# Attention layer of a three-layer fp32 block: softmax rows turned by VectorE in 32x32 blocks and moved by transfers inside SBUF, with the division on ScalarE

## The reference, cut to what matters

```
h  = rmsnorm(x) * (1 + scale) + shift;  proj = h @ w_in      # q, k, v, z
A, heads 0-7 (dense):    s = rope(norm(q)) @ [rope(norm(k)), k_ctx].T * d**-0.5    # 512 x 768
                         o = softmax(s) @ [v, v_ctx]
B, heads 8-15 (window):  each 128-row block of q sees up to 3 neighbouring 128-key blocks, masked,
                         the 256 context keys, and a sink logit that only enters the total
y = concat(oA, oB) * silu(z);  x = x + gate * rmsnorm(y @ w_out)
```

## Time and profile before

| | busy us | share of the span | instructions |
|---|---|---|---|
| span 2534.0 us; median time 2536.99 us | | | 30108 |
| TensorE matmuls (PE) | 2497.7 | 99% | 11975 |
| TensorE weight loads (PEld) | 2020.2 | 80% | 11975 |
| VectorE (DVE) | 1623.8 | 64% | 2444 |
| ScalarE (ACT) | 973.6 | 38% | 1549 |
| GpSimd (POOL) | 110.7 | 4% | 117 |

### The profile page before, as it was taken

How to read it: one execution, slowest core, us unless ns; L and a number is a source line. 1 busy time by engine, 2 the same in 40 slices (tenths; PEclk the granted TensorE clock), 3 DMA queues, 4 the chain that set the end, 5 groups by cost and what they waited for, 6 DMA issues and landing times.

```text
span 2534.0 us, 30108 instructions
## 1 busy us (share of the span) xinstructions
PE 2497.7 (99%) x11975; PEld 2020.2 (80%) x11975; DVE 1623.8 (64%) x2444; ACT 973.6 (38%) x1549; POOL 110.7 (4%) x117
## 2 busy tenths in 40 slices
PE   7999999999999999999999999999999999999999
PEld 4789777777777887888888887888888787887887
DVE  4456776677776768776776768456365577656532
ACT  4232444444444333432434333445455432333421
POOL 0000000000000114000000113000000000000000
PEclk8999999999999999999999999999999999999999
DMA  9955433434433754666645754323222245532342
GB/s 350 336 193 185 127 110 121 125 125 133 132 101 136 258 180 157 208 200 211 200 162 175 249 175 158 111 76 91 80 87 84 75 151 169 175 112 89 123 154 83
DMA packets 293133, 390.58 MB, mean 154 GB/s; under 512 B 11698, under 2 KB 221234, under 8 KB 289154
## 3 DMA queue, kind: packets, MB, share of 16 engines
q1 hardware_dynamic: 287184, 355.84, 43.5%
q0 software_dynamic: 5808, 32.84, 3.5%
q10 hardware_dynamic: 2, 0.00, 0.0%
HBM read 371.85 MB, written 16.78 MB: 153 GB/s over the span
## 4 chain that ended last, share of the span: by engine, by line
PE 89%; DVE 5%; DMA 2%; ACT 2%; issue 1%; SPq 1%; POOL 0%; DVEq 0%; ACTq 0%; POOLq 0%
PE G L2151 74%; PE OB L2151 6%; PE S L2151 6%; PE TB L2154 2%; PE TB L2151 1%; DMA MRAW<-in_ev_mod_w 1%; DMA MORE<-in_ev_mod_w 1%; DVE WLO L1634 1%; DVE MACC L1640 1%; DVE TT L1634 1%; ACT PB L1445 1%; DVE SM L1862 0%; SPq L1129 0%; PE OB L2154 0%; DVE Y L1634 0%
## 5 line engine op out<-in xcount | busy, mean ns | idle before, releaser
L2151 PE MATMUL G<-HHI,WLO 128*128 128x512 f32 x2560 | 1001.0, 391 | 0.0
L2151 PE MATMUL G<-HHI,WHI 128*128 128x512 f32 x1964 | 801.8, 411 | 0.5 <-DVE CLO L1640 0.5
L2151 PE MATMUL G<-HLO,WHI 128*128 128x512 f32 x1928 | 753.2, 391 | 1.6 <-DVE HLO L1640 1.4
L2151 PEld LDWEIGHTS G<-HHI,WLO 128*128 128x128 f32 x2560 | 480.7, 188 | 104.3
L1272 ACT ACTIVATE WHI<-RAW 128x1024 fp32r<-128x1024 f32 x282 | 297.5, 1056 | 560.9 <-PE G L2151 501.6
L1634 DVE TENSOR_TENSOR WLO<-RAW,WHI 128x1024 fp32r<-128x1024 f32 x282 | 344.5, 1222 | 234.9 <-ACT WHI L1272 233.0
L2151 PEld LDWEIGHTS G<-HHI,WHI 128*128 128x128 f32 x1964 | 370.9, 189 | 80.3 <-issue 6.7
L2151 PEld LDWEIGHTS G<-HLO,WHI 128*128 128x128 f32 x1928 | 363.1, 188 | 79.7 <-issue 6.7
L1640 DVE SCALAR_TENSOR_TENSOR MACC<-MWIDE,SC,MACC 128x512 f32<-128x512 f32 x420 | 320.4, 763 | 39.2 <-DMA MWIDE<-in_w_ada 12.8
L2151 PE MATMUL G<-HHI,WHITA 128*128 128x512 f32 x536 | 215.0, 401 | 0.0
L2151 PE MATMUL G<-HLO,WHITA 128*128 128x512 f32 x536 | 209.2, 390 | 0.0
(11 more groups left out here) (347 smaller groups left out, 3060.7 us busy)
## 6 DMA issues: line engine op xcount, KB each, us to landing
RAW<-in_w_in SPq DMA_DIRECT2D x128, 512.0 KB, 3.7
MWIDE<-in_od_mod_w SPq DMA_DIRECT2D x96, 512.0 KB, 4.1
MWIDE<-in_w_ada SPq DMA_DIRECT2D x96, 512.0 KB, 4.6
RAW<-in_ev_w_in SPq DMA_DIRECT2D x80, 512.0 KB, 3.5
RAW<-in_od_w_in SPq DMA_DIRECT2D x64, 512.0 KB, 3.9
MWIDE<-in_ev_mod_w SPq DMA_DIRECT2D x32, 512.0 KB, 3.8
RAW<-in_ev_w_out SPq DMA_DIRECT2D x32, 512.0 KB, 3.3
RAW<-in_od_w_out SPq DMA_DIRECT2D x32, 512.0 KB, 3.3
```

The lines of the kernel that those rows point to most:

```text
L2151: return e.o.matmul(o, l, r, start=start, stop=stop, skip_group_check=True)
```

## The change

The transposes of PB leave TensorE. ScalarE, not VectorE, multiplies a tile by the inverse totals, in place. VectorE then turns each 32x32 block of the tile in place (`transpose` of a 24x32 view). When half a head (two tiles, 256 rows) is turned, SP issues 16 transfers from PB to PT: for each quarter of 32 source partitions `a_` and each residue `r` of the 32-key groups, one of 32 partitions x 6 x 64 elements, that is 192 pieces of 256 B. For 16 heads these are 512 transfers. Columns of PT within a head now lie in another order (quarter, tile, row), which `pv` and `gate` undo with strided views. PB becomes one tensor for a whole head, a half of which may be written again when its transfers have landed. An exponential of a B head with qt < 2 goes out in two instructions, context keys and near keys. Tiles 4 to 7 of a pair come two steps later, and `pv` comes 11 steps after the head's last tile in place of 7. GpSimd's descriptor memory is halved, and WHI gets an ordinary fourth buffer (WHITA and WHIY with their waits go).

```diff
-    WHI3 = [place(f"WHI{i}", [P, 4, 256], F32R)[0] for i in range(3)]
+    WHI = [place(f"WHI{i}", [P, 4, 256], F32R)[0] for i in range(3)]
...
-    PB = [scratch(f"PB{i}", [P, 768], F32, 24 * K1 + i * 3 * K1) for i in range(2)]
+    PB = scratch("PB", [P, 24, P], F32, 24 * K1)
...
+    WHI.append(scratch("WHI3", [P, 4, 256], F32R, 52 * K1))
...
-                later(3 * n, "rows", n)
+                later(3 * n + (2 if n > 3 and p < 7 else 0), "rows", n)
...
-                        later(t + 4 + late, "turn", h, qt, n, 0, not two)
...
-                            later(t + 7, "pv", h)
+                        if qt == 1:
+                            later(t + (6 if i else 4), "turn", h, 0)
+                        elif qt == 3:
+                            later(t + 4, "turn", h, 1)
+                            later(t + 11, "pv", h)
...
+    def p_rows(qt, kt0, kt1):
+        return PB[:, 4 * kt0:4 * kt1, 32 * qt:32 * qt + 32]
...
@@ sp_program @@
+            elif stage == "turn":
+                h, half = a
+                e.wait_ge(v_sm, (h, 2 * half + 1, "turned"))
+                if h:
+                    e.wait_ge(p_pv, h - 1)
+                for a_ in range(4):
+                    src = PB[32 * a_:32 * a_ + 32, :, 64 * half:64 * half + 64].rearrange("p (k r) n -> p k r n", r=4)
+                    for r in range(4):
+                        e.o.dma_start(PT[32 * r:32 * r + 32, :, P * a_ + 64 * half:P * a_ + 64 * half + 64],
+                                      src[:, :, r, :]).then_inc(*ptd[half].up(h, by=16))
...
@@ ScalarE, stage softmax @@
+                if h:
+                    e.wait_ge(ptd[qt // 2], h - 1)
...
+                e.wait_ge(v_sm, (h, qt, "inverse"))
+                cp(p_rows(qt, kt0, 6), p_rows(qt, kt0, 6), SM[:, i + 1:i + 2]).then_inc(*a_exp.up((h, qt, "p")))
@@ VectorE, stage softmax @@
-                e.wait_ge(v_sm, (h, qt, "inverse"))
-                ts(PB[n % 2][:, lo:768], PB[n % 2][:, lo:768], rs, None, MUL).then_inc(*v_sm.up((h, qt, "p")))
+                rows = p_rows(qt, jobs[0][0], 6)
+                e.wait_ge(a_exp, (h, qt, "p"))
+                e.o.transpose(rows, rows).then_inc(*v_sm.up((h, qt, "turned")))
...
@@ TensorE, stages turn and pv @@
-                for x, (j, c0) in enumerate(jobs):
-                    t = tr(bank[:, x * P:(x + 1) * P], PB[n % 2][:, c0:c0 + P])
...
+                e.wait_ge(ptd[0], h)
+                e.wait_ge(ptd[1], h)
...
-    nc = bacc.Bacc("TRN2", target_bir_lowering=False, num_devices=1)
+    nc = bacc.Bacc("TRN2", target_bir_lowering=False, num_devices=1, dynamic_dma_scratch_size=8192)
```

More of the change, by code:

```diff
@@ L185, in build @@
     KHI.append(scratch("KHI3", [P, 768], F32R, 0))
-    QLO = scratch("QLO", [P, 2, SEQ], F32R, 42 * K1)
+    QLO = scratch("QLO", [P, 2, SEQ], F32R, 48 * K1)
     LS2 = [LS, LSB]
@@ L213, in build @@
     xnd = [sig(f"xn{i}") for i in range(6)]
+    ptd = [sig(f"pt{i}") for i in range(2)]
     back = [sig(f"back{i}") for i in range(4)]
@@ L216, in build @@
     last = [sig(f"last{i}") for i in range(4)]
-    sigs = raw + mraw + [par, sel, cst, rope, tri, spill, rcd, dkd] + xnd + back + outd + last
+    sigs = raw + mraw + [par, sel, cst, rope, tri, spill, rcd, dkd] + xnd + ptd + back + outd + last
     def on_chip(*names):
@@ L285, in build @@
     units += out_units(T["od_w_out"][0])
-    third = len(units)
     for p in range(4):
@@ L304, in build @@
         first_chunk.append(first_chunk[-1] + len(u))
[L306 to L317, removed]
     nat = [("c", 0), ("c", 1)] + [("x", i) for i in range(4)]
@@ L731, in pair_task @@
                         put("softmax", h, qt, n)
-                        two = len(score_jobs(h, qt)[1]) > 4
-                        late = 1 if a[0] % 4 == 0 else 0
-                        later(t + 4 + late, "turn", h, qt, n, 0, not two)
-                        if two:
-                            later(t + 5 + late, "turn", h, qt, n, 1, True)
-                        if qt == 3:
-                            later(t + 7, "pv", h)
+                        if qt == 1:
[3 more added lines that the diff above has]
+                            later(t + 11, "pv", h)
                     elif what == "pv":
@@ L745, in pair_task @@
                 yield
+                if p == 7 and t > 28 and last_y < KT - 1:
+                    put("y_split", 1, last_y, h_unit)
+                    last_y += 1
             if p == 7:
-                for k in range(12, KT):
-                    put("y_split", 1, k, h_unit)
-                    yield
+                put("y_split", 1, KT - 1, h_unit)
+                yield
         def first_splits(layer):
@@ L1082, in q_root_of, with by_block @@
         return QROOT[:, h % 2 * 4 + qt:h % 2 * 4 + qt + 1]
-    def runs_of(part):
-        runs = []
-        for x, (j, c0) in enumerate(part):
-            if runs and runs[-1][1] + runs[-1][2] == j:
-                runs[-1][2] += 1
-            else:
-                runs.append([x, j, 1])
-        return runs
+    def p_rows(qt, kt0, kt1):
+        return PB[:, 4 * kt0:4 * kt1, 32 * qt:32 * qt + 32]
+    def by_block(t):
+        return t.rearrange("p (b j) -> p b j", j=32)
     def operand(kind, layer, k):
@@ L1750, in dve_program @@
                 e.wait_ge(a_whi, i)
-                tt(WLO[i % NR][:, :, :], RAW[i % NR][:, :, :], f(whi(i)[:, :, :]), SUB).then_inc(*v_wlo.up(i))
+                tt(WLO[i % NR][:, :, :], RAW[i % NR][:, :, :], f(WHI[i % NS][:, :, :]), SUB).then_inc(*v_wlo.up(i))
             elif stage == "mod_acc":
@@ L2161, in keep_busy @@
             for _ in range(count):
-                mm(G[pair][0][:, :], whi(i)[:, 0, 0:P], HHI[:, KT - 1, :], True, True)
+                mm(G[pair][0][:, :], WHI[i % NS][:, 0, 0:P], HHI[:, KT - 1, :], True, True)
         def token_sums(x, tile, start):
@@ L2304, in pe_program @@
                 layer, u, i, c, t_, pair, last, final = a
-                wh, wl = whi(i), WLO[i % NR]
+                wh, wl = WHI[i % NS], WLO[i % NR]
                 bank = (G[pair] + [OB])[t_ // 2]
```

96 lines of the change are left out of this document (38 added, 58 removed).

## The result

The kernel after takes 2684.67 us (median, 2680.24 to 2687.1), the kernel before beside it 2536.73 us (2535.18 to 2538.44). The ratio is 1.0576, with an interval of 1.0563 to 1.0589: 148 us slower. The forecast was 2565 us, with a range up to 2600. The direction was right and the time was 120 us too short.

What follows compares the result with a forecast made beforehand. TensorE bounds the heads now and loses 37 us; VectorE gets 79 us more against 51.4 us of room and becomes the limit. 2534.0 + 27.6 = 2561.6, with 3 us around it about 2565 us, range 2508 to 2600.

Steps and rivals of the forecast that it cites:

- What bounds the kernel before, and what leaves TensorE: Heads: TensorE busy 277.2 of 280 and 267.2 of 270 us; 336 transposes at 0.11 us leave, 37 us.
- VectorE's new work: Heads' tiles: waiting for ScalarE's multiplication, then turning, adds 41.6 us in A and 37.4 in B, 79 together.
- The sum of 28 us for VectorE: Heads: 79 us more work against 51.4 us of room leaves VectorE needing 27.6 us more than 550.
- SP issues 512 transfers; at 0.37 us each they are 189 us: SP's queue in the heads: a group of 16 takes 5.9 us, SP waits 503 of 550 us; costed at nothing.
- An MWIDE load: Weight loads on SP: issued 11 us ahead, 1.6 us of cover left; if gone, 1 to 2 us in 32 groups.
- So `pv` doesn't wait: Heads: transfers land 13.8 us after a head's last score, and `pv` comes 15.2 us after it.
- ScalarE's wait for the transfers of the head before: ScalarE writing PB: those transfers were issued at least 9.7 us earlier, so costed at nothing.
- The transfers' own cost: DMA engines in the heads: 21 ns per 256 B piece, so a half head takes 4.0 us per engine.
- Rival 3: Transfers land late and `pv` waits, from about 24 ns per piece; 2682 us at 61 ns, 2578 at 40; chance 0.13.
- Rival 1: Heads: VectorE has the room, TensorE keeps the path, all 37 us are won, 2500 to 2503 us; chance 0.20.
- the signs I had named: Heads: TensorE busy about 89%, VectorE's WHI and OB waits nearly vanish, `pv` never waits for transfers' landing.

Runs made afterwards that it cites:

- split: Kernel after with 8 of each 16 transfers issued by SP and 8 by GpSimd: 2572.48 us, 1.0142 of the kernel before.
- few: Kernel after, but from the second head on only 4 of each half head's 16 transfers are issued: 2578.23 us, 1.0166 of the kernel before.
- mwpool: Kernel after with the first layer's MWIDE loads issued by GpSimd, SP keeping all 512 transfers: 2598.09 us, 1.0240 of the kernel before.
- spload: Kernel before plus 512 transfers of the same shape on SP into spare memory nobody reads: 2578.66 us, 1.0164 of the kernel before.
- halfpieces: Kernel after with 96 pieces in place of 192 per transfer from the second head on: 2678.85 us, 1.0558 of the kernel before.

## Why the prediction was wrong, step by step

**What bounds the kernel before, and what leaves TensorE.** Right. All kernels with the transposes gone have 336 matmuls fewer. The 37 us they give back weren't measured by themselves.

**VectorE's new work.** Right in its terms. For 768 columns the wait in front of the turning was put at 1.00 us and is 1.00 (48.2 us in 48 times), and the turning was put at 0.954 us and takes 0.978. ScalarE's multiplication was put at 0.92 us:

```profile
L1865 DVE STREAM_TRANSPOSE PB<-PB 128x768 f32<-128x768 f32 x48 | 47.0, 978 | 48.2 <-ACT PB L1267 48.2
L1865 DVE STREAM_TRANSPOSE PB<-PB 128x640 f32<-128x640 f32 x8 | 6.8, 845 | 7.2 <-ACT PB L1267 7.2
L1865 DVE STREAM_TRANSPOSE PB<-PB 128x512 f32<-128x512 f32 x8 | 5.7, 712 | 6.3 <-ACT PB L1267 6.3
```
```profile
L1267 ACT ACTIVATE PB<-PB,SM x64: 721/936/942, 265.9 to 915.7; 128x768 f32<-128x768 f32 x48, 128x640 f32<-128x640 f32 x8, 128x512 f32<-128x512 f32 x8
```

It is 0.936. One term was sized wrongly: in 16 of the B tiles the turned view spans all six blocks of keys, so 48 tiles and not 32 are turned at full width, which the code states (`p_rows(qt, kt0, 6)`) and I read past. For eight of them that is 0.98 + 1.00 us against 0.71 + 0.79 at 512 columns, for the other eight against 0.85 + 0.90 at 640, together about 6 us.

**The sum of 28 us for VectorE.** Nearly right as a size, and not as a place. Where the transfers are out of the way, 36 us (split) and 42 us (few) are left. TensorE's waits in front of S and for QLO are 48.0 us in split, where the forecast had 65. But from first to last exponential the A heads take 257.5 us before and 258.7 in split, and the B heads 236.2 and 273.2. The forecast had some 12 us of the need in A (41.6 - 29.9) and 16 in B (37.4 - 21.5); the runs show about 1 and 37. Nor did the room go as counted: in split VectorE still waits 24.5 us for WHI. So the size came out near partly by luck, and what makes the B heads dearer is open. The granted clock stood at 0.99 and 0.93 from 250 to 550 and from 550 to 850 us of that kernel; whether the clock took time there, or TensorE had it to spare, no run tells apart.

**"SP issues 512 transfers; at 0.37 us each they are 189 us ... A group of 16 takes 5.9 us and holds up the loads behind it."** This step failed, first in its price. The earlier trace rows show an issue that stands alone. In the trace of before there are also pairs, and the second of a pair takes longer:

```profile
804.44 0.37 SPq L1135 DMA_DIRECT2D RAW<-in_ev_w_out  x1
804.86 0.54 SPq L1143 DMA_DIRECT2D MWIDE<-in_od_mod_w  x1
```

This row of before was to be had. It is still short of the 0.61 us in a streak, but it would have said that 0.37 us is the lower bound and not the price. With 0.65 us the 512 issues are 331 us, and a group is 10.3 to 11.6 us in place of 5.9.

**"An MWIDE load ... 5.9 + 3.5 us to landing leave 1.6 us. If that cover is gone VectorE waits once per group."** This step failed more deeply. The cover was gone, and I priced its loss as a load that comes 1 to 2 us late, and in the sum at nothing. I did not ask what SP's queue itself waits for. An MWIDE load waits for VectorE, and the groups behind it wait too, so a late VectorE makes late transfers, a late `pv`, late transposes of MACC and a later VectorE. The sum "2.5 + 1.9 + 5.9 + 3.5 = 13.8 us after the score, `pv` 15.2 us later" assumed that SP stands ready when a tile is turned. The earlier trace rows said that SP stood waiting for 503 of 550 us. I took them for free time, and they are the time in which a new instruction behind them can't start. Mwpool shows the size of this: 87 us. In place of "So `pv` doesn't wait" the trace has 87.4 us of waits in front of `pv`.

**ScalarE's wait for the transfers of the head before.** Put at nothing, since they were issued at least 9.7 us earlier. They were planned so; in fact they leave late, and ScalarE waits 26.8 us in seven places (rows above).

**The transfers' own cost.** Right, as far as a difference of two pages can tell. A piece was put at 21 ns. In the page after, the queue is busy for 46.0% of 2678.5 us:

```profile
q1 hardware_dynamic: 393680, 381.04, 46.0%
```

Against the earlier trace rows that is 0.460 x 16 x 2678.5 - 0.435 x 16 x 2534 = 2077 us for 106,496 more packets, 19.5 ns each (spload gives 19.3 in the same way). This is an estimate, since it takes the other packets as unchanged. "DMA: Bandwidth & Descriptors" of the Trainium skill says under "Issuing engines are not separate DMA queues" that several issuing engines only save the issue time, which is usually small beside the DMA. The first half fits halfpieces in that the bytes weren't what counted, but mwpool gave 87 us for some 25 us of issues, so an issuing queue costs its order too. The second doesn't hold here: a transfer of 48 KB lands in 2.0 us, its issue takes 0.65 us of the sequencer, and taking half of the issues off one queue gave 112 us.

**The rivals.** Rival 3 had the right place, `pv` at the head of TensorE's queue, and nearly the right time (2682), for a price that is wrong: it hung on the cost of a piece, which is 19.5 ns and below the 24 from which it decided. The time agrees by chance. Rival 1, that VectorE has the room, is refuted by split and few. That the kernel got slower wasn't luck: both are slower than before, with one wait of 5.0 us for a transfer in front of `pv` in few and none in split. Of the signs I had named, the fall of TensorE's busy share to 89% came out at 80%, VectorE's waits for WHI didn't vanish (34.0 us in 20 places), and "the landing of the transfers is never what `pv` waits for" was false.

## What to carry to other kernels

An instruction that is added to an in-order queue costs its place, not only its time: ask what the instruction ahead of it waits for, and whether that engine waits, through others, for the new instruction. That a queue stands waiting for 90% of its time (503 of 550 us here) says nothing about its room for work that must start on time. Where new work stands behind loads that wait for another engine, moving those loads can give back far more than their issue time (87 us for 25 us here). Cutting the new work into parts gave nothing, but the parts were placed no further apart than they are long, so check the distance in the plan against the time of a part. Price a DMA's issue from rows in which issues follow each other.

## What the hardware showed that I had not expected

- On SP one issue takes 0.37 us alone, 0.51 to 0.54 us as the second of a pair, and 0.61 us with 0.04 between in a streak, with 192 pieces or with 96. On GpSimd the same transfers take 0.572 us each.
- Pieces of 256 B inside SBUF cost about 19.5 ns of a DMA engine, an estimate from the difference of the two pages.
- Behind a wait of 6.68 us TensorE was granted 0.53 of its clock for 3.3 us, and the wide products of `pv` took 829 ns on the mean, against 596 where nothing waited.
- VectorE turns 128x768 fp32 elements in 32x32 blocks in 0.978 us, 128x640 in 0.85 us and 128x512 in 0.71 us.
